# One input tile moved to the neighbouring step, gate transcendentals split by tokens, and the queries' factors issued later, in a chunked linear recurrence

## What is computed

```python
def forget_terms(z, lb):
    log_f = jnp.logaddexp(jnp.log(lb), jnp.log1p(-lb) + jax.nn.log_sigmoid(z))
    k = (1 - lb) * jax.nn.sigmoid(-z)
    return k, log_f

# per head and direction, over the tokens:
#   S_t = diag(f_t) S_{t-1} + k_t v_t^T,   o_t = S_t^T q_t
q, zf, zb, i, g = split_cols(modulate(x, shift, scale) @ w_in, widths)
```

## Time and profile before

| | |
|---|---|
| median of 3 runs | 2301.48 us (2299.9 to 2304.84) |
| the profiled execution | 2302.98 us, span of its trace 2301.0 us |
| TensorE busy over the span | 93% |
| mean granted clock of TensorE | 0.974 of full speed |
| the recurrence (steps 0 to 7) | about 563 to 990 us of the span |

### The profile page before, as it was taken

How to read it: one execution, slowest core, us unless ns; L and a number is a source line. 1 busy time by engine, 2 the same in 40 slices (tenths; PEclk the granted TensorE clock), 3 DMA queues, 4 the chain that set the end, 5 groups by cost and what they waited for, 6 DMA issues and landing times. The chain is left out here.

```text
span 2301.0 us, 27282 instructions
## 1 busy us (share of the span) xinstructions
PE 2137.7 (93%) x11287; PEld 1712.2 (74%) x11287; DVE 1045.9 (45%) x1685; ACT 664.4 (29%) x1040; POOL 805.2 (35%) x429
## 2 busy tenths in 40 slices
PE   4999988989999999986998889999998999999998
PEld 3887777866685758976756778888887678888886
DVE  1114664673565655569985651111127674111114
ACT  3223323325545454732103441000013443000011
POOL 1421112321343334328100025544544234554553
PEclk7999999999999999997999999999999999999999
DMA  9233123443111111121111122223322222322322
GB/s 295 68 109 99 40 74 92 111 128 92 37 37 37 37 37 38 56 83 60 55 37 37 56 73 92 92 92 104 98 91 87 79 94 79 103 92 92 109 84 82
DMA packets 183114, 187.41 MB, mean 81 GB/s; under 512 B 25728, under 2 KB 162256, under 8 KB 182864
## 3 DMA queue, kind: packets, MB, share of 16 engines
q1 hardware_dynamic: 173040, 175.42, 24.8%
q10 hardware_dynamic: 9376, 8.16, 1.3%
q0 software_dynamic: 576, 2.10, 0.2%
HBM read 183.56 MB, written 2.10 MB: 81 GB/s over the span
## 5 line engine op out<-in xcount | busy, mean ns | idle before, releaser
L3011 POOL TENSOR_TENSOR weights_lo<-weights_raw,weights_hi 128x2048 fp32r<-128x2048 f32 (+1 forms) x101 | 457.4, 4530 | 864.7 <-ACT weights_hi L1429 668.6
L698 PE MATMUL ring<-input_hi,weights_hi 128*128 128x512 f32 x784 | 305.4, 390 | 4.1 <-POOL weights_lo L3011 4.0
L700 PE MATMUL ring<-input_hi,weights_lo 128*128 128x512 f32 x784 | 305.0, 389 | 0.0
L699 PE MATMUL ring<-input_lo,weights_hi 128*128 128x512 f32 x784 | 305.0, 389 | 0.0
L2837 DVE CAST weights_hi<-weights_raw 128x2048 fp32r<-128x2048 f32 (+1 forms) x72 | 87.6, 1217 | 366.2 <-PE ring L700 173.9
L2998 POOL TENSOR_TENSOR h_w<-h_p 128x512 f32<-128x512 f32 x56 | 80.9, 1445 | 338.9 <-PE ring L1013 201.6
L698 PEld LDWEIGHTS ring<-input_hi,weights_hi 128*128 128x128 f32 x784 | 147.1, 188 | 36.2 <-issue 5.8
L989 PE MATMUL obank<-acts,weights_raw 128*128 128x512 f32 x384 | 172.4, 601 | 0.0
L700 PEld LDWEIGHTS ring<-input_hi,weights_lo 128*128 128x128 f32 x784 | 147.1, 188 | 30.6
L699 PEld LDWEIGHTS ring<-input_lo,weights_hi 128*128 128x128 f32 x784 | 147.2, 188 | 30.4
L998 PE MATMUL obank<-weights_raw,acts 128*128 128x256 f32 x640 | 142.1, 379 | 0.0
(11 more groups left out here) (465 smaller groups left out, 4375.2 us busy)
## 6 DMA issues: line engine op xcount, KB each, us to landing
weights_raw<-in_w_ada SPq DMA_DIRECT2D x24, 1024.0 KB, 5.3
weights_raw<-in_ffn_w_gate SPq DMA_DIRECT2D x22, 1024.0 KB, 5.4
weights_raw<-in_ffn_w_up SPq DMA_DIRECT2D x22, 1024.0 KB, 5.4
weights_raw<-in_ffn_w_down SPq DMA_DIRECT2D x16, 1024.0 KB, 5.0
weights_raw<-in_w_in_c SPq DMA_DIRECT2D x12, 1024.0 KB, 5.2
weights_raw<-in_w_in_ab SPq DMA_DIRECT2D x9, 1024.0 KB, 7.6
weights_raw<-in_w_in_c SPq DMA_DIRECT2D x16, 512.0 KB, 5.3
weights_raw<-in_ev_w_in SPq DMA_DIRECT2D x8, 1024.0 KB, 5.5
```

Of the source, the lines that this page charges most:

```text
L698: pe.matmul(o, hi[:, k, ms], xh[:, k, t0:t0 + n], start=k == 0, stop=False)
L699: pe.matmul(o, hi[:, k, ms], xl[:, k, t0:t0 + n], start=False, stop=False)
L700: last = pe.matmul(o, lo[:, k, ms], xh[:, k, t0:t0 + n], start=False, stop=k == KD - 1)
L3011: pool.tensor_tensor(W_LO[slot][:, 0:kt, :], WR[:, slot, 0:kt, :], w_hi[:, 0:kt, :], ALU.subtract).then_inc(sem("w_lo"), 1)
```

## The change

It does four things, all within the recurrence.

- The six tiles of `i` are grouped as (0), (1, 2), (3, 4), (5) in place of three pairs. The first group moves from the odd step to the even step before it, between the two parts of q. Steps 0, 2, 4 then have 11 halves, share (2, 2, 2, 1, 1, 2, 1, 0), and steps 1, 3, 5 have 11 too, with the same share. Steps 6 and 7 are as before.
- |z|, its small exponential, the log and the join are each cut into latents (128x1024) and context (128x512). |z| of the latents is issued ahead of level 5's operand, its exponential behind level 5's and ahead of slot 2. The context pieces and both logs stand where the whole stood.
- `state_factors` ends with the state keys' factors. The queries' factors (L1668, L1669) become `query_factors` with a semaphore of their own, issued after the exponential of the next step's level 0, which has moved ahead of slot 5. VectorE's `query_operand` waits for the new semaphore.
- The same in the part ahead of step 0: the pieces and the four groups of `i` in turn.

```diff
+        TOKENS = (slice(0, L), slice(L, LT))
+        I_TILES = ((0,), (1, 2), (3, 4), (5,))
+        def halves_of(unit):
+            return (1,) if unit[0] == "i" and len(I_TILES[unit[2]]) == 1 else (0, 1)
 def c_slots(st):
-            if hb + 1 < HEADS // HH:
-                units += [("iq"[j == 0], hb + 1, part) for part in range(2 if j == 0 else 3)]
+            if hb + 1 == HEADS // HH:
+                units += G_UNITS[3:] if j else G_UNITS[:3]
+            elif j == 0:
+                units += [("q", hb + 1, 0), ("i", hb + 1, 0), ("q", hb + 1, 1)]
             else:
-                units += G_UNITS[3:] if j else G_UNITS[:3]
-            halves = [unit + (half,) for unit in units for half in range(2)]
+                units += [("i", hb + 1, part) for part in range(1, len(I_TILES))]
+            halves = [unit + (half,) for unit in units for half in halves_of(unit)]
-                share = (2, 2, 2, 1, 0, 2, 1, 0) if len(units) == 5 else (2, 2, 2, 1, 1, 2, 2, 0)
+                share = (2, 2, 2, 1, 1, 2, len(halves) - 10, 0)
...
 ScalarE
-            def small_exp(st):
-                t = HT_[st % 2]
-                act.wait_ge(sem("hg_abs"), st + 1)
-                act.activation(t[:, :, :], t[:, :, :], ACT.Exp, scale=-1.0).then_inc(sem("hg_small"), 1)
+            def small_exp(st, part):
+                t = HT_[st % 2][:, :, TOKENS[part]]
+                act.wait_ge(sem("hg_abs"), 2 * st + part + 1)
+                act.activation(t, t, ACT.Exp, scale=-1.0).then_inc(sem("hg_small"), 1)
...
+            def query_factors(st):
+                b = st % 2
                 for c in range(TL):
                     cs = slice(c * P, (c + 1) * P)
                     act.activation(HT_[b][:, 1, cs], HP[b][:, 1, cs], ACT.Exp, scale=-1.0, bias=PL[b][:, 1, c:c + 1])
-                act.activation(HT_[b][:, 0, 0:L], HP[b][:, 0, 0:L], ACT.Exp).then_inc(sem("hg_exps"), 1)
+                act.activation(HT_[b][:, 0, 0:L], HP[b][:, 0, 0:L], ACT.Exp).then_inc(sem("hg_query_exps"), 1)
...
                 level_exp(7 * st + 5)
+                if more:
+                    small_exp(st + 1, 0)
                 between(2)
                 if more:
-                    small_exp(st + 1)
-                    log1p(st + 1)
+                    small_exp(st + 1, 1)
+                    for part in range(2):
+                        log1p(st + 1, part)
                 level_exp(7 * st + 6)
                 between(3)
                 if more:
                     keys(st + 1)
                 between(4)
                 if more:
                     state_factors(st + 1)
+                    level_exp(7 * st + 7)
+                    query_factors(st + 1)
                 between(5)
                 if more:
-                    level_exp(7 * st + 7)
                     level_exp(7 * st + 8)
 VectorE
-                dve.wait_ge(sem("hg_ln"), st + 1)
-                dve.scalar_tensor_tensor(out=HT_[b][:, :, :], in0=HZ[b][:, :, :], scalar=0.0, in1=HT_[b][:, :, :],
+                for part, ts in enumerate(TOKENS):
+                    dve.wait_ge(sem("hg_ln"), 2 * st + part + 1)
+                    dve.scalar_tensor_tensor(out=HT_[b][:, :, ts], in0=HZ[b][:, :, ts], scalar=0.0, in1=HT_[b][:, :, ts],
...
 query_operand
                 dve.wait_ge(*product_emptied(("q", hb, 1)))
+                dve.wait_ge(sem("hg_query_exps"), st + 1)
...
+                if more:
+                    abs_z(st + 1, 0)
                 level_operand(7 * st + 5)
                 if more:
-                    abs_z(st + 1)
+                    abs_z(st + 1, 1)
                 level_scores(st, 3)
```

More of the change, by code:

```diff
@@ L963, in c_pieces @@
                 return cols(wc, C_COLS[kind] + key * WC)
-            C_PARTS = {"z": 3, "q": 2, "i": 3, "g": 2}
+            C_PARTS = {"z": 3, "q": 2, "i": len(I_TILES), "g": 2}
             c_weights, c_release = {}, {}
             def product(unit):
-                product_half(unit, 0)
-                product_half(unit, 1)
+                for half in halves_of(unit):
+                    product_half(unit, half)
             def product_half(unit, half):
                 kind, key, part = unit
-                if half == 0:
+                if half == halves_of(unit)[0]:
                     if part == 0:
@@ L995, in product_half @@
                 else:
-                    t = 2 * part + half
+                    t, at = 2 * part + half, half
+                    if kind == "i":
+                        at = half if len(I_TILES[part]) == 2 else 0
+                        t = I_TILES[part][at]
                     for k in range(KD):
-                        last = pe.matmul(ps[:, half * WC:(half + 1) * WC], HT[:, k, t * P:(t + 1) * P], wv[:, k, :],
+                        last = pe.matmul(ps[:, at * WC:(at + 1) * WC], HT[:, k, t * P:(t + 1) * P], wv[:, k, :],
                                          start=k == 0, stop=k == KD - 1)
@@ L1064, in _ @@
             mod_next(15)
-            product(("i", 0, 1))
-            product(("i", 0, 2))
+            for part in range(1, len(I_TILES)):
+                product(("i", 0, part))
             mod_turn(1, 11)
@@ L1092, in _ @@
                 levels(st, 1)
-                pe.wait_ge(*product_emptied(("i", hb, 2)))
+                pe.wait_ge(*product_emptied(("i", hb, len(I_TILES) - 1)))
                 for part, js in enumerate((range(0, 4), range(4, 5))):
@@ L1627, in take_product @@
                 elif kind == "i":
-                    ins = act.activation(HI[k % 2][:, 2 * part:2 * part + 2, :], two, ACT.Copy)
+                    t0, n = I_TILES[part][0], len(I_TILES[part])
+                    ins = act.activation(HI[k % 2][:, t0:t0 + n, :], two[:, 0:n, :], ACT.Copy)
                 else:
@@ L1635, in _, with log1p @@
             DEC = [SM[:, 128 + 12 * b:140 + 12 * b] for b in range(2)]
-            def small_exp(st):
-                t = HT_[st % 2]
-                act.wait_ge(sem("hg_abs"), st + 1)
-                act.activation(t[:, :, :], t[:, :, :], ACT.Exp, scale=-1.0).then_inc(sem("hg_small"), 1)
[L1643 to L1647, removed]
+            def small_exp(st, part):
+                t = HT_[st % 2][:, :, TOKENS[part]]
+                act.wait_ge(sem("hg_abs"), 2 * st + part + 1)
+                act.activation(t, t, ACT.Exp, scale=-1.0).then_inc(sem("hg_small"), 1)
+            def log1p(st, part):
+                t = HT_[st % 2][:, :, TOKENS[part]]
+                act.wait_ge(sem("hg_small"), 2 * st + part + 1)
+                act.activation(t, t, ACT.Ln, bias=ONES[:, 0:1]).then_inc(sem("hg_ln"), 1)
             PL = [SM[:, 352 + 12 * b:364 + 12 * b].rearrange("p (h c) -> p h c", h=HH) for b in range(2)]
@@ L1664, in state_factors @@
                     cs = slice(c * P, (c + 1) * P)
-                    act.activation(HZ[b][:, 0, cs], HP[b][:, 0, cs], ACT.Exp, scale=-1.0, bias=PL[b][:, 0, c:c + 1])
+                    last = act.activation(HZ[b][:, 0, cs], HP[b][:, 0, cs], ACT.Exp, scale=-1.0, bias=PL[b][:, 0, c:c + 1])
+                last.then_inc(sem("hg_exps"), 1)
+            def query_factors(st):
+                b = st % 2
                 for c in range(TL):
@@ L1701, in _ @@
             keys(0)
-            small_exp(0)
-            log1p(0)
+            for part in range(2):
+                small_exp(0, part)
+            for part in range(2):
+                log1p(0, part)
             take_product(("q", 0, 1))
@@ L1708, in _ @@
             level_exp(0)
+            query_factors(0)
             level_exp(1)
             mod_next(15)
-            take_product(("i", 0, 1))
-            take_product(("i", 0, 2))
+            for part in range(1, len(I_TILES)):
+                take_product(("i", 0, part))
             mod_columns(1, 11)
@@ L2255, in _, with abs_z @@
             PL = [SM[:, 352 + 12 * b:364 + 12 * b].rearrange("p (h c) -> p h c", h=HH) for b in range(2)]
[L2257 to L2260, removed]
+            def abs_z(st, part):
+                z = HZ[st % 2][:, :, TOKENS[part]]
+                dve.wait_ge(*product_emptied(("z", st, 1 + part)))
+                dve.scalar_tensor_tensor(out=HT_[st % 2][:, :, TOKENS[part]], in0=z, scalar=-1.0, in1=z,
                                          op0=ALU.mult, op1=ALU.max).then_inc(sem("hg_abs"), 1)
@@ L2403, in _ @@
             MS = SM[:, 160:192].rearrange("p (t h) -> p t h", t=TL)
-            abs_z(0)
+            abs_z(0, 0)
+            abs_z(0, 1)
             log_f_and_sums(0)
```

4 lines of the change are left out of this document (2 added, 2 removed).

## The result

| | median, us | runs | ratio to the kernel before (95% interval) |
|---|---|---|---|
| before, beside it | 2301.72 | 4 | |
| changed | 2287.89 (2281.68 to 2289.47) | 4 | 0.993 (0.9915 to 0.9944) |

The changed kernel is faster by 0.7%, 13.8 us by the medians. The forecast was 2282.6 us, in a range from 2279.5 to 2291.5, and 18.85 us of gain. The profiled execution of the changed kernel took 2286.36 us, its span is 2284.3.

What follows compares the result with a forecast made beforehand. TensorE, busy 93% of the span, was taken as the bound, idle in the recurrence only ending steps 0, 2, 4. Holes of 19.15 us less 0.3 gave 18.85, off 2301.48: 2282.6 us, range 2279.5 to 2291.5.

Steps and rivals of the forecast that it cites:

- The price of the holes: Ends of steps 0, 2, 4: TensorE loses 5.33, 6.95 and 6.87 us against undisturbed lengths, together 19.15 us.
- The split: ScalarE and VectorE, abs to join in two pieces: the log ends 1.8 us earlier, bounds 1.3 to 2.1.
- rival (a): Even steps: first q's Silu up to 0.7 us late for the second q's bank; 2285 to 2292 us, chance 0.11.
- The added table load: ScalarE, ahead of the first q's Silu: load 1.29 us plus Silu 0.60, done at 717.7, bank slack 0.7 us.
- Rival (b): New ScalarE table switch costs twice 1.29 us: Silu 0.6 us late, 1.8 us in three steps, 2284.4 us, chance 0.02.
- The queries' factors: Moved behind level 0's exponential: in even steps slack 2.7 us for state keys, 1.6 for level 0; odd steps 2.2.
- Ahead of step 0: The group of one tile ends 3.46 us sooner, so TensorE waits about 0.3 us for ScalarE's row, bounds 0 and 1.5.
- Rival (c): The pieces' fixed costs eat the split and the tile merely fills the hole: 2294.4 or 2291.1 us, chance 0.05.
- Rival (d): Slower: the first q's Silu stays late, second q 6.75 us late, 20.3 us in three steps; 2310 us, chance 0.04.
- Rival (e): A wait in the odd steps eats four fifths of the gain, leaving the time within 0.2%; chance 0.04.
- I subtract from the median: Whole kernel: the 18.85 us gain is taken from the median 2301.48, not the profiled 2302.98, giving 2282.6 us.
- the prediction's last sign: Total time: if it moves by less than 15 us, one of the slacks is wrong.

Runs made afterwards that it cites:

- the last experiment: Changed kernel with VectorE's gate row diagonal and its wait moved behind the first two level operands: 2274.89 us, ratio 0.9883; the same again 2278.87 us, 0.9901.
- The later measurements: The changed kernel run twice more, unaltered, against the kernel before: 2284.38 us, ratio 0.9923, and 2283.85 us, ratio 0.9921.
- the second sigmoid: Changed kernel with the keys' sigmoid done twice by ScalarE in each step but the first: 2290.31 us, ratio 0.9946.

## Why the prediction was right, point by point

- **The price of the holes** held: 19.15 us by comparing lengths, 19.26 measured between step 0's and step 7's transposes. Less the 0.15 at the start of step 0 it is 19.11. The idle time of the holes alone, 12.2 us (1.98 and 1.14 at the end of step 0, then twice 1.84, 0.24 and 2.48), would have missed a third.
- **An idle time that the prediction overlooked**: it says that the idle time sits at one place, the ends of steps 0, 2 and 4. There is also the wait at the start of step 0, 3.26 us before and 3.11 after. The change does not touch it, so the sum is not hurt; but 19.15 us was not the most that could be taken from the recurrence, as the last experiment's 4.7 us show.
- **The tile costs nothing in TensorE's work**: steps of 51.26 and 51.19 us, forecast 51.2. No wait for a chunk of weights in the steps.
- **The split** brought the log's end forward by 1.7 us (1.8), and without it the bank wait of rival (a) appears, 0.96 us against 1.0 to 1.1. Rival (a) itself did not come: 0.66 us of slack.
- **The added table load** costs 1.30 us ahead of the Silu (load at 709.64, Silu at 710.94), as in the earlier trace rows. Rival (b) is out. By the rule of the Trainium skill, ScalarE: Activation LUTs, What ACT_TABLE_LOAD costs, a switch is 2.66 us in all; by an estimate from that figure the Silu would have ended at 712.90, 0.70 us late for the bank. The trace does not agree.
- **The queries' factors**: needed, but their place was mis-sized. The step "level 0's operand at about 725.7, for 727.29: slack 1.6" came out at 0.35. It had VectorE's two products at 0.69 and 0.68 us; they ran beside GpSimd's level arguments, and took 1.39 and 1.10. In the odd steps the slack is 1.0, not 2.2; that either part alone would do there, the prediction did not see. Nothing waited, so the sum did not notice.
- **Ahead of step 0**: from the first turn of the modulation rows (L759, in the changed kernel L768) to the transposes 24.15 us before (539.00 to 563.15) and 24.50 after (537.89 to 562.39), so 0.35 us lost, forecast 0.3.
- **Rival (c)** is refuted by the trace without split: the pieces' fixed costs do not eat the split. **Rival (d)** needed 6.3 us of lateness; ScalarE put back by 1.5 us made a wait of 0.74. **Rival (e)**: the odd steps have no wait.
- **The total** missed by 5 us at first, 2287.89 against 2282.6. The weak step is "I subtract from the median", with "behind the recurrence everything ... moves with it": it let nothing happen outside the recurrence. There the same kernel's executions differ by several us, and the stretch right behind it took some 2 us more in every trace of the changed kernel. The later measurements missed by 1.8 and 1.3 us (2284.38 and 2283.85). The upper part of the range was meant for rivals that did not come; the first median fell there by the spread of executions. So the prediction's last sign, that under 15 us of gain one of the slacks is wrong, misled: it moved by 13.8, and no slack had run out.

## What to carry to other kernels

Price a hole by the length of the same work undisturbed, not by its idle time; here the rest, the fall of the clock above all, added half as much again. When work is moved into a hole, follow what each of its consumers' queues does next: here the moved tile pulled a Silu with its table load ahead of the critical factors, and only the split made room for it. And when the medians can't separate two versions (the later queries' factors, 2.35 us), the pitch of a repeated step in one trace can.

## What the runs showed of the hardware that I had not expected

Waits of 0.52 to 1.19 us in the steps, 21 of them over five kernels, did not lower TensorE's granted clock, which stayed at 1.00, and cost their idle time and 0.25 to 0.35 us more. In the kernel before, the clock fell to 1.2 GHz only behind longer ones: at the end of step 0 behind 1.98 us (0.72 over 612.78 to 618.88), in steps 2 and 4 not behind 1.84 (1.00 over 720.41 to 725.24) but behind 2.48 (0.82 over 729.03 to 738.52). The length of the wait does not decide it alone: behind the 3.11 us in step 0 the work slowed in every trace of the changed kernel, but not in the one with the second sigmoid. I had charged up to 2.4 us of clock for each wait in the rivals, and too much in two expectations.

VectorE's product of 128x512 took 0.68 us alone and up to 1.56 beside GpSimd's arguments, and an argument of 128x256 took 2.15 us instead of 0.61 beside VectorE's product of the state keys (L2312, 715.67 to 717.60). From the changed kernel, two arguments of GpSimd, then a product of VectorE while GpSimd did nothing:

```profile
715.95 2.15 POOL L3030 TENSOR_TENSOR h_w<-h_p 128x256 f32<-128x256 f32 x1
718.06 1.07 POOL L3028 TENSOR_TENSOR h_w<-h_p 128x512 f32<-128x512 f32 x1
726.17 0.68 DVE L2331 TENSOR_TENSOR h_w<-h_w,h_k 128x512 f32<-128x512 f32 x1
```

That the one engine delays the other is read from their overlap in time; no run changed GpSimd's work by itself. A slack that two such engines share is worth reading from a trace, not from the lone durations.
